# Inverse roots of the norms as a power on GpSimd, in place of ScalarE's root and VectorE's reciprocal

## What is computed

```python
def rms_norm(x, gain=None):
    xf = x.astype(jnp.float32)
    y = xf * lax.rsqrt(jnp.mean(xf * xf, axis=-1, keepdims=True) + EPS)
    if gain is not None:
        y = y * gain.astype(jnp.float32)
    return y.astype(x.dtype)

def modulate(x, shift, scale):
    return rms_norm(x) * (1 + scale) + shift
```

## Time and profile before

| | us |
|---|---|
| median of 3 runs | 3560.04 |
| lowest and highest | 3558.72, 3570.94 |
| the profiled execution | 3564.15 |
| its span | 3562.8 |
| TensorE busy | 3245.5 |
| VectorE busy | 2063.8 |
| ScalarE busy | 1664.8 |
| GpSimd busy | 221.6 |

### The profile page before, as it was taken

The page is one execution under the profiler, slowest core; times in us unless marked ns, Lnnn a source line. Parts: engine busy times, 40 slices in busy tenths (PEclk is TensorE's granted clock), DMA queues, the critical chain, the costliest instruction groups (busy, mean ns, idle before and its releaser), DMA issues.

```text
span 3562.8 us, 51089 instructions
## 1 busy us (share of the span) xinstructions
PE 3245.5 (91%) x19360; PEld 2768.5 (78%) x19360; DVE 2063.8 (58%) x4132; ACT 1664.8 (47%) x3572; POOL 221.6 (6%) x290
## 2 busy tenths in 40 slices
PE   7998999998899777996899999987699779999999
PEld 4745677786699766985689999987598658999998
DVE  2233433335665665598666666656558876666665
ACT  2244322223654335419755555543451685555554
POOL 0021000000200160000000000006100000000000
PEclk9999899997999787999999999978699999999999
DMA  5402344432156322440355555543053115655554
GB/s 207 177 1 83 128 174 166 151 109 72 48 181 179 108 78 65 149 160 1 105 185 185 187 185 188 185 137 106 12 178 131 65 36 184 189 184 184 189 185 153
DMA packets 135059, 479.91 MB, mean 135 GB/s; under 512 B 15520, under 2 KB 17440, under 8 KB 134048
## 3 DMA queue, kind: packets, MB, share of 16 engines
q1 hardware_dynamic: 132944, 471.26, 40.6%
q10 hardware_dynamic: 1872, 5.38, 0.4%
HBM read 475.53 MB, written 1.05 MB: 134 GB/s over the span
## 4 chain that ended last, share of the span: by engine, by line
PE 84%; DVE 8%; issue 4%; ACT 3%; DMA 1%; SPq 0%; ACTq 0%; DVEq 0%
PE psum L706 14%; PE psum L708 14%; PE psum L707 14%; PE psum L2370 7%; PE psum L2371 7%; PE psum L2372 7%; PE psum L2292 6%; PE psum L2216 4%; PE psum L557 3%; PE psum L999 2%; PE psum L354 1%; PE psum L571 1%; DVE conv_part L1457 1%; DVE w_lo L248 1%; PE psum L1009 1%
## 5 line engine op out<-in xcount | busy, mean ns | idle before, releaser
L248 DVE TENSOR_TENSOR w_lo<-raw,w_hi 128x512 fp32r<-128x512 f32 x1472 | 1005.9, 699 | 821.1 <-ACT w_hi L239 793.7
L239 ACT ACTIVATE w_hi<-raw 128x512 fp32r<-128x512 f32 x1472 | 894.8, 625 | 882.3 <-PE psum L708 495.8
L706 PE MATMUL psum<-x_hi,w_hi 128*128 128x256 f32 x2096 | 604.8, 289 | 30.7 <-DVE w_lo L248 23.4
L707 PE MATMUL psum<-x_lo,w_hi 128*128 128x256 f32 x2096 | 600.6, 287 | 0.0
L708 PE MATMUL psum<-x_hi,w_lo 128*128 128x256 f32 x2096 | 597.2, 285 | 0.0
L706 PEld LDWEIGHTS psum<-x_hi,w_hi 128*128 128x128 f32 x2096 | 401.9, 192 | 43.6 <-DVE w_lo L248 25.7
L2370 PE MATMUL psum<-w_hi,wt_hi 128*128 128x512 f32 x1024 | 407.3, 398 | 6.5 <-DVE wt_lo L2428 6.5
L707 PEld LDWEIGHTS psum<-x_lo,w_hi 128*128 128x128 f32 x2096 | 404.0, 193 | 8.2
L2371 PE MATMUL psum<-w_lo,wt_hi 128*128 128x512 f32 x1024 | 407.0, 397 | 0.0
L2372 PE MATMUL psum<-w_hi,wt_lo 128*128 128x512 f32 x1024 | 407.0, 397 | 0.0
L708 PEld LDWEIGHTS psum<-x_hi,w_lo 128*128 128x128 f32 x2096 | 406.8, 194 | 0.0
(11 more groups left out here) (315 smaller groups left out, 4652.4 us busy)
## 6 DMA issues: line engine op xcount, KB each, us to landing
raw<-in_v SPq DMA_DIRECT2D x256, 512.0 KB, 4.2
raw<-in_u SPq DMA_DIRECT2D x190, 512.0 KB, 3.4
raw<-in_mod_w SPq DMA_DIRECT2D x96, 512.0 KB, 4.2
raw<-in_w_gate_up SPq DMA_DIRECT2D x88, 512.0 KB, 4.8
u_raw<-in_u SPq DMA_DIRECT2D x66, 512.0 KB, 3.5
raw<-in_w_in SPq DMA_DIRECT2D x40, 512.0 KB, 4.0
raw<-in_w_down SPq DMA_DIRECT2D x32, 512.0 KB, 3.6
raw<-in_w_peer SPq DMA_DIRECT2D x32, 512.0 KB, 4.2
```

The costliest lines, as they stand in the source:

```text
L239: self.nc.scalar.activation(self.hi[:, m % 4, :], self.half(m), ACT.Copy).then_inc(self.rounded[m % 4], 1)
L248: self.nc.vector.tensor_tensor(self.lo[:, m % 4, :], self.half(m), self.hi[:, m % 4, :], ALU.subtract).then_inc(self.ready[m % 4], 1)
L706: pe.matmul(out[:, 0:width], hi[:, w], x_hi, start=(c == 0), stop=False)
L707: pe.matmul(out[:, 0:width], hi[:, w], x_lo, start=False, stop=False)
```

## The change

25 of the 35 sets get their inverse root in another way; `heads` and `ln` of the mixers keep the old one (`by_pool=False`). For the others ScalarE does nothing. VectorE waits for all sums, writes sum / n + eps of every set into `mean_col` (`vector_means`), then for each set waits for GpSimd and copies into `spread`. GpSimd raises the column to the power of -1/2 in place, with a constant -0.5 that VectorE sets at the start. GpSimd's list gets these steps in program order, ahead of the clearing of `pad` in the mixer, and ahead of or behind its attention.

```diff
@@ class Setup
-        self.made = k.named("constants_made").take(3)
-        self.done = [self.made.after(3)]
+        self.made = k.named("constants_made").take(4)
+        self.done = [self.made.after(4)]
...
+        nc.vector.memset(k.power, -0.5).then_inc(self.made.sem, 1)
@@ class InvRms
     def scalar_root(self):
+        if self.by_pool:
+            return
...
-    def vector_invert(self):
+    def vector_means(self):
         k, dve = self.k, self.k.nc.vector
+        dve.wait_ge(*self.sums.full(self.n))
+        at = 0
+        for chunks, width, group in self.sets:
+            t, ng = width // P, P // group
+            sums = self.sums.tensor[:, 4 * at:4 * (at + t)].rearrange("p (t g) -> p t g", g=4)
+            dve.tensor_scalar(k.mean_col[:, at:at + t, 0:ng], sums[:, :, 0:ng], 1.0 / (group * len(chunks)), EPS,
+                              ALU.mult, ALU.add).then_inc(self.sums.read.sem, 1)
+            at += t
+
+    def gpsimd(self):
+        k, pool = self.k, self.k.nc.gpsimd
         at = 0
         for s, (_, width, group) in enumerate(self.sets):
             t, ng = width // P, P // group
             col = k.mean_col[:, at:at + t, 0:ng]
-            dve.wait_ge(*self.sums.emptied(s + 1))
-            dve.reciprocal(col, col).then_inc(self.turned.sem, 1)
-            dve.wait_ge(*self.turned.after(s + 1))
+            pool.wait_ge(*self.sums.emptied(s + 1))
+            pool.tensor_tensor(col, col, k.power.unsqueeze(2).to_broadcast([P, t, ng]),
+                               ALU.pow).then_inc(self.raised.sem, 1)
+            at += t
+
+    def vector_invert(self):
+        k, dve = self.k, self.k.nc.vector
+        if self.by_pool:
+            self.vector_means()
+        at = 0
+        for s, (_, width, group) in enumerate(self.sets):
+            t, ng = width // P, P // group
+            col = k.mean_col[:, at:at + t, 0:ng]
+            if self.by_pool:
+                dve.wait_ge(*self.raised.after(s + 1))
+            else:
+                dve.wait_ge(*self.sums.emptied(s + 1))
+                dve.reciprocal(col, col).then_inc(self.turned.sem, 1)
+                dve.wait_ge(*self.turned.after(s + 1))
@@ class EvenMixer
     def gpsimd(self):
+        self.modulated.gpsimd()
+        self.normed.gpsimd()
         self.att.gpsimd()
+        self.modulated_ffn.gpsimd()
@@ class Mixer
     def gpsimd(self):
+        self.normed.gpsimd()
         self.branches.clear(self.start)
...
         self.att.gpsimd()
+        self.sub.gpsimd()
+        self.groups.gpsimd()
```

More of the change, by code:

```diff
@@ L112, in __init__ @@
         self.ident, self.group32, self.group64, self.swap8, self.swap16 = (self.cmat[:, j, :] for j in range(5))
-        vectors = self.sb("gvec", [P, 8 + 2 * G_COLS + 2], 52224)
+        vectors = self.sb("gvec", [P, 8 + 2 * G_COLS + 3], 52224)
         self.gvec = vectors[:, 0:8 + 2 * G_COLS]
-        self.eps, self.warmed = vectors[:, 8 + 2 * G_COLS:9 + 2 * G_COLS], vectors[:, 9 + 2 * G_COLS:]
+        self.eps, self.warmed = vectors[:, 8 + 2 * G_COLS:9 + 2 * G_COLS], vectors[:, 9 + 2 * G_COLS:10 + 2 * G_COLS]
+        self.power = vectors[:, 10 + 2 * G_COLS:]
         self.stats = self.sb("stats", [P, 40], 53184)
@@ L439, with __init__ @@
 class InvRms:
-    def __init__(self, k, sets, banks, reads):
-        self.k, self.sets = k, sets
+    def __init__(self, k, sets, banks, reads, by_pool=True):
+        self.k, self.sets, self.by_pool = k, sets, by_pool
         self.n = sum(len(chunks) for chunks, _, _ in sets)
@@ L448, in __init__ @@
         self.sums = k.bank[6].use(written=self.n, read=len(sets))
-        self.turned = k.named("inverse_made").take(len(sets))
+        self.turned = k.named("inverse_made").take(0 if by_pool else len(sets))
+        self.raised = k.named("means_raised").take(len(sets) if by_pool else 0)
         self.spread = k.named("inverse_spread").take(len(sets))
@@ L575, with __init__ @@
 class Norm(InvRms):
-    def __init__(self, k, items, banks=(7,)):
+    def __init__(self, k, items, banks=(7,), by_pool=True):
         super().__init__(k, [(src, width, group) for _, src, _, width, group, _ in items], banks,
-                         [len(src) for _, src, _, _, _, _ in items])
+                         [len(src) for _, src, _, _, _, _ in items], by_pool)
         self.jobs = [(s, c, dst[c], src[c], gain[c], pairs and pairs[c])
@@ L1884, in gpsimd @@
     def gpsimd(self):
+        self.modulated.gpsimd()
         self.att.gpsimd()
+        self.modulated_ffn.gpsimd()
+        self.last.gpsimd()
 class Mixer(Between):
@@ L1944, in __init__ @@
         self.heads = Norm(k, [head(proj[:, 6:8, :], 32, dq), head(proj[:, 8:10, :], 32, k.gain(l, G_DK)),
-                              head(proj[:, 16:18, :], HD, mq), head(mk[:], HD, k.gain(l, G_MK))], (4, 5, 7, 6))
+                              head(proj[:, 16:18, :], HD, mq), head(mk[:], HD, k.gain(l, G_MK))], (4, 5, 7, 6),
+                          by_pool=False)
         self.second = ScalarProjection(k, io[f"w_in{l}"], [0, 1, 10, 11], [DC], xs, LAT, place)
@@ L1952, in __init__ @@
         cs = [conv[:, c, :] for c in range(2)]
-        self.ln = Norm(k, [(cs, cs, columns(k.gain(l, G_LNG, 2), 2), LAT, P, None)], (7,))
+        self.ln = Norm(k, [(cs, cs, columns(k.gain(l, G_LNG, 2), 2), LAT, P, None)], (7,), by_pool=False)
         self.branches.reserve()
@@ L2566, in gpsimd_program @@
     def gpsimd_program(self):
+        hold(self.k.nc.gpsimd, self.setup.done)
         self.even.gpsimd()
         self.odd.gpsimd()
-        for layer in self.layers[0::2]:
+        for layer in self.layers:
             layer.gpsimd()
```

## The result

| | before | after |
|---|---|---|
| median, us | 3560.04 (11 runs) | 3572.20 (11 runs) |
| lowest and highest | 3553.97, 3570.94 | 3564.65, 3579.92 |
| profiled execution | 3564.15 | 3579.92 |

The ratio is 1.0029, with a 95% interval of 1.0016 to 1.0041: the change costs 6 to 15 us, 10 in the middle of that (the medians lie 12.2 apart). The forecast was 3573. The profiled execution of after is the slowest of its 11, so the 15.8 us between the two profiled ones are no measure of the change; the single holes are.

The account below looks back on a forecast made before the run. TensorE bounds the kernel (91% busy, 84% of the chain), so only 14 norm holes count. 3.7 + 3.0 + 2.9 + 3.0 - 1.6 + 1.7 = +12.7 us, median 3573, range 3560 to 3606.

Parts of the forecast that it names:

- The power: GpSimd's inverse root: 0.2 us per element on 0.36 fixed, so 0.76 us for 2 elements, 1.16 for 4, 1.96 for 8.
- 256 columns: Six holes, four single and two pairs: 1.46 us against 0.84, +0.62 each, +3.7 together.
- 512 columns: Three holes, in `modulated_ffn`, `modulated` and the even layer's pair: 2.00 us against 1.00, +3.0 together.
- `sub`: Two norms of 8 elements: hole 2.83 us against 1.36, +2.9 together, the table load's gain included.
- `groups`: Two norms of five sets, powers in a row: first apply at 4.47 us against 2.97, +1.5 each, +3.0.
- The pairs: Two pairs of 256 columns: second power free behind TensorE's 1.23 us of spreading, so only +0.62 each.
- The first norm: Without the root in ScalarE's queue `row` fills earlier; TensorE spreads at 46.86 in place of 48.44, -1.6 us.
- The clock at `sub`: The longer hole drops TensorE to 1.2 GHz; 8 spreading products take 2.07 us, not 1.23: +0.84 twice, +1.7.
- The table loads: Eight ScalarE loads of 1.283 us go; six lie under sums, two at `sub` are worth some 0.25 us each.
- A dear power: At all 25 sets: power's arithmetic over 0.28 us per element crosses 0.5%; at 0.5 us, +32, 3592; chance 0.35.
- A slow first power: First norm: GpSimd's first power delayed, some 5 us crosses 0.5%; with about 6 us, 3579; chance 0.08.
- Tables worth their time: Eight ScalarE table switches cost full time: 12 us back gives 3561, 21 us with drain 3552; chance 0.05.

Follow-up runs that it names:

- experiment 6: Changed kernel with GpSimd multiplying the mean by 0.001 in place of the power; 3564.37 us, ratio 1.0003 to before.
- experiment 8: Changed kernel with GpSimd clearing `pad` ahead of the powers of the mixer's first norm; 3572.25 us, ratio 1.0016 to before.
- experiment 9: Kernel of before, with ScalarE's weight roundings and fill of `row` ahead of its root in the first norm; 3560.38 us, ratio 1.0000.
- experiment 2: Changed kernel with only the very first norm using GpSimd, all others root and reciprocal; 3563.11 us against 3560.61 before, ratio 1.0007.
- experiment 3: Changed kernel with all but the very first norm using GpSimd; 3571.96 us, ratio 1.0042 to before.
- experiment 7: Changed kernel with ScalarE's 8 table loads and 14 warm-ups put back, no root following; 3569.68 us, ratio 1.0024 to before.
- experiment 5: Changed kernel with a second power, to the power of 1, after every power; 3599.36 us against 3564.66 before, ratio 1.0096.
- experiment 1: Changed kernel run again with no edit, for its time and a second trace; 3574.38 us, ratio 1.0039 to before.

## Why the prediction was right

The sum was +12.7, the medians lie 12.2 apart, and the ratio gives 10 (6 to 15). The mechanism is the one that was predicted, powers in 14 places that nothing covers. That the forecast came within 1 us of the median is luck: the terms below add up to 10.5, several were too large and one too small, and the interval is 9 us wide. Point by point:

- **The power**: shape right, size a little too high. 0.2 us per element on 0.36; measured 0.16 on 0.38. The multiply of experiment 6 takes 0.20 to 0.21 with the same operands; so 0.48 of the 0.70 for 2 elements, and 1.45 of the 1.66 for 8, are what a power takes beyond a multiply. The intercept from long instructions in the earlier trace rows agreed only by chance. The lower end rested on a misreading: 0.53 us was not GpSimd's shortest. The same trace has copies of 64x256 at 0.47 and clearings of one element at 0.10.
- **Handovers**: 0.09 to GpSimd is 0.08; 0.1 back is 0.04. Together too high by 0.07 in each hole.
- **256 columns**: +0.62 each; measured +0.48 in the singles, 1.9 us for four. **512 columns**: +1.0; measured +0.78, 2.3 for three. **`sub`**: 2.83 for the hole; measured 2.57, +2.4 for two. **`groups`**: 4.47; measured 3.84, +1.7 for two; five in a row take 0.67 each, as they overlap a little.
- **The pairs** were the step that failed, though small. I called the second power free behind TensorE's 1.23 us, which it is (two powers are over at 1202.46), but did not see that the clearing of `pad`, moved behind the powers, now runs exactly beside VectorE's second copy. I had counted GpSimd's queue and its next work, but not what runs beside it on VectorE. +1.1 each in place of +0.62, of which experiment 8 gives back 0.6. The trace of before had a sign of it: at `heads` of layer 0 a copy into `spread` of 512 columns takes 1.35 us (from 1297.36) beside an add of GpSimd (1297.34 to 1298.42), and the two after it 0.43.
- **The first norm**: 46.86 forecast, 46.78 measured, and the mechanism is shown by experiment 9 without GpSimd. About 1 us more seems to come in the stage behind it, but it lies in waits that differ between executions (experiment 9). Whether any of the gain reaches the end of the program stays open: experiments 2, 3 and 9 can't tell 2 us from none, and experiment 2's interval only just lets a gain in.
- **The clock at `sub`**: right in after, 2.08 and 2.03 us for the eight products, and not certain: in the other execution of the same kernel they take 2.07 in layer 0 and 1.70 in layer 1, and in experiment 2, with the old hole of 1.35 us, 1.66 in layer 0. The earlier trace rows show 0.89 over the products, not over the hole; the hole itself, 1367.8 to 1369.1, has 1.00. So what this term is worth varies, 0.5 to 0.9 us at each `sub`.
- **The table loads**: right that they lay under cover. Experiment 7 puts all of them back at no cost that shows.

The measured terms are 1.9 + 2.2 + 2.3 + 2.4 + 1.7 - 1.7 + 1.7 (clock) = 10.5. That agrees with the interval of 6 to 15, so what is left over needs no further cause; nor is it excluded that there is one of a few us. The same sum for the other kernels, from the end of the sums to the first apply over the 14 norms, against before, is 32.5 us for experiment 5 (the ratio gives 34), 12.5 for 3 (15), 9.2 for 8 (6), -0.9 for 6 (+1) and -2.1 for 9 (0). In each the sum lies within the interval of the ratio.

**The rivals.** A dear power (0.35) would have begun at 0.28 us per element. A slow first power: the first takes 1.01 us, the five of its size 1.015 in the mean; it is excluded. Tables worth their time: excluded by experiment 7. My 0.40 for slower by over 0.5% was the width of one unknown, the arithmetic, and it was near: 64 elements stand on the path, so 0.25 us for each in place of 0.16 would have added 5.8 us to the 12.2 between the medians and reached 0.5%. The power twice over went to nearly 1%.

No version beat both kernels by more than can be measured. What the traces support is the kernel of before with the fill ahead of the root, though no time shows its gain.

## What to carry to other kernels

An operation that moves to an idle engine is not free if everybody waits for it: price it at the places where nothing covers it, element by element, and test by doubling it. A table load in front of a wait that outlasts it cost nothing here; look at the wait behind it before counting loads. When work is moved in an engine's queue, look at what will then run beside it on the others: the clearing of `pad`, moved by two powers, slowed a copy that TensorE waited for. And when a change shortens one engine's queue, look at what else stood behind the removed step: here the only gain of the change was that, and it was to be had by a reordering alone.

## What the runs showed of the hardware beyond that

- A multiply of 2 to 8 elements takes GpSimd 0.203 to 0.215 us, a power 0.70 to 1.66. A one-element copy had taken 0.53 in the earlier trace rows; of the same two instructions in after one takes 0.53 and the other 0.19, and in experiment 1 both take 0.53. A short row of GpSimd's is no floor for another instruction.
- VectorE's copy of 256 float32 takes 0.29 us alone and beside a GpSimd power (all five at `groups`), and 1.11 to 1.25 beside a GpSimd clearing of 1152 columns, in every trace that has them side by side. The Trainium skill (GPSIMD Engine Reference, Specifications) says that the two share their SBUF interfaces and names VectorE's 2-port modes as a case of contention; a copy at 0.29 us for 256 elements beside one held for 0.83 more fits that, though no row tells the mode of a copy. The rows show in addition that the small powers do not disturb.
- The 6 us that the Trainium skill (GPSIMD Engine Reference, Instruction dispatch) gives for the first call to a freshly loaded kernel on GpSimd do not show at the power: 1.01 us at its first use.
- TensorE's granted clock over the same one-column products differs between executions of one kernel: 0.52 and 0.65 in after, with 2.5 us between them.
